# Second projection of a fused kernel: its first weight pieces are loaded one block earlier and split ahead of the latents' normalisation

## The reference

```
h = x * (1.0 + sc1) + sh1
p = h @ w_in[i]
mla_o = mla_group(p[..., :MLA_IN], cos, sin, ...)          # MLA_IN = 416
rwkv_o, v_i = rwkv7_group(p[..., MLA_IN:], ...)            # 1792 features
mix = jnp.concatenate([mla_o, rwkv_o], axis=-1) @ w_o[i]
x = layer_norm(ALPHA * x + (1.0 + gt1) * mix, ...)
x = layer_norm(ALPHA * x + (1.0 + gt2) * moe_ffn(h2, ...), ...)
```

## Time and profile before

| | us |
|---|---|
| median of three runs | 1998.43 |
| lowest, highest | 1998.28, 2002.58 |
| the profiled execution's own time | 1993.24 |
| its span, first to last instruction | 1991.5 |
| end of the entry block, PE's last instruction | 438.8 |
| second projection, from there to PE's last instruction | 438.8 to 562.3 |

### The profile page before, as it was taken

How to read it: one execution, slowest core, us unless ns; L and a number is a source line. 1 busy time by engine, 2 the same in 40 slices (tenths; PEclk the granted TensorE clock), 3 DMA queues, 4 the chain that set the end, 5 groups by cost and what they waited for, 6 DMA issues and landing times.

```text
span 1991.5 us, 27259 instructions
## 1 busy us (share of the span) xinstructions
PE 1887.4 (95%) x9418; PEld 1507.1 (76%) x9418; DVE 1576.8 (79%) x1614; ACT 1212.8 (61%) x1246; POOL 437.3 (22%) x381
## 2 busy tenths in 40 slices
PE   7999989988999879799999999999999999999997
PEld 6766656775767677788888888888888888888884
DVE  5763353773466569889999999999999999999996
ACT  5545564423464322367777777777777777777773
POOL 4535543010053332241111111111111111111110
PEclk9999998999999899799999999999999999999999
DMA  7535442414101023689999999999999999999994
GB/s 204 167 111 186 138 143 78 163 34 105 53 1 33 22 86 130 241 315 377 389 398 389 399 396 391 392 381 397 380 398 392 384 393 381 399 384 399 387 371 156
DMA packets 180403, 525.08 MB, mean 264 GB/s; under 512 B 34531, under 2 KB 52019, under 8 KB 180339
## 3 DMA queue, kind: packets, MB, share of 16 engines
q1 hardware_dynamic: 156882, 458.27, 60.5%
q0 software_dynamic: 21376, 65.95, 11.5%
q10 hardware_dynamic: 2080, 0.01, 0.1%
HBM read 499.06 MB, written 25.12 MB: 263 GB/s over the span
## 4 chain that ended last, share of the span: by engine, by line
PE 57%; DVE 2%; issue 0%; POOLq 0%; POOL 0%; DVEq 0%
PE banks L3419 53%; PE banks L3407 3%; PE banks L3413 1%; PE banks L3483 0%; DVE expert_weights L3757 0%; DVE x_tokens L3753 0%; DVE weights_lo L3553 0%; DVE x_tokens L3764 0%; DVE x_tokens L3636 0%; PE banks L3540 0%; PE banks L3504 0%; PE banks L3474 0%; DVE u_lo L3589 0%; DVE rows_lo L3583 0%; DVE member L3616 0%
## 5 line engine op out<-in xcount | busy, mean ns | idle before, releaser
L3553 DVE TENSOR_TENSOR weights_lo<-expert_weights,weights_hi 128x2048 fp32r<-128x2048 f32 x384 | 876.7, 2288 | 65.9 <-ACT weights_hi L3793 61.9
L3793 ACT ACTIVATE weights_hi<-expert_weights 128x2048 fp32r<-128x2048 f32 x384 | 738.6, 1926 | 264.2 <-PE banks L3419 252.0
L3419 PE MATMUL banks<-weights_hi,rows_hi 128*128 128x512 f32 x1024 | 319.1, 393 | 0.0
L3419 PE MATMUL banks<-weights_hi,rows_lo 128*128 128x512 f32 x1024 | 315.5, 389 | 0.0
L3419 PE MATMUL banks<-weights_lo,rows_hi 128*128 128x512 f32 x1024 | 273.8, 389 | 0.0
L3419 PEld LDWEIGHTS banks<-weights_hi,rows_hi 128*128 128x128 f32 x1024 | 189.8, 188 | 44.9 <-issue 7.3
L3419 PEld LDWEIGHTS banks<-weights_hi,rows_lo 128*128 128x128 f32 x1024 | 192.3, 188 | 40.4
L3419 PEld LDWEIGHTS banks<-weights_lo,rows_hi 128*128 128x128 f32 x1024 | 192.3, 188 | 39.9
L3419 PE MATMUL banks<-weights_hi,u_hi 128*128 128x512 f32 x512 | 160.9, 395 | 1.4 <-DVE u_lo L3589 1.4
L3419 PE MATMUL banks<-weights_hi,u_lo 128*128 128x512 f32 x512 | 157.9, 390 | 0.0
L3419 PE MATMUL banks<-weights_lo,u_hi 128*128 128x512 f32 x512 | 136.9, 389 | 0.0
(11 more groups left out here) (608 smaller groups left out, 2824.0 us busy)
## 6 DMA issues: line engine op xcount, KB each, us to landing
expert_weights<-in_exp_w SPq DMA_DIRECT2D x384, 1024.0 KB, 10.3
enter_rows<-in_ada_w POOLq DMA_DIRECT2D x24, 1024.0 KB, 5.7
w_in_landing<-in_w_in SPq DMA_DIRECT2D x16, 384.0 KB, 3.2
second_landing<-in_w_in SPq DMA_DIRECT2D x12, 512.0 KB, 3.6
x_tokens<-in_x SPq DMA_DIRECT2D x8, 512.0 KB, 6.2
w_in_landing<-in_w_in SPq DMA_DIRECT2D x8, 512.0 KB, 3.6
rwkv_room<-in_w_o SPq DMA_DIRECT2D x8, 512.0 KB, 7.6
w_in_landing<-in_w_in SPq DMA_DIRECT2D x12, 256.0 KB, 3.8
```

The lines of the kernel that those rows point to most:

```text
L3419: last = nc.tensor.matmul(c.banks[:, bank + n, :], left[:, 2 * q + kk, :], right[:, q, kk * FF + n * 512:kk * FF + (n + 1) * 512], start=s ...
L3553: nc.vector.tensor_tensor(w_lo[:, ch % SPLIT, :], c.raw[:, ch % RAW if place is None else place, :], w_hi[:, ch % SPLIT, :], ALU.subtract) ...
L3793: nc.scalar.activation(w_hi[:, ch % SPLIT, :], c.raw[:, ch % RAW if place is None else place, :], ACT.Copy).then_inc(hi_ready.sem, 1)
```

## The change

The entry block's SP list gets a wait for `products` at 8 and then issues pieces 0 to 3 of the second projection. Their landing place is set aside at a fixed address; each of the two places takes two 256 KB pieces side by side, and there are four semaphores instead of two. In the second projection, SP issues w_uv, w_uk and then pieces 4 to 15; the four loads of w_uq move to the end of POOL's loads, with a semaphore of their own, and the first value waits for w_uv and w_uk alone. PE's ten unused products go, and quarter 0 comes first; the latents are given after m = 7, and every later use six quarters later than before (values after 9, 11, 13, 15 instead of 3, 5, 7, 9, and so on to the norms after 46 to 52). ACT runs `high(0)` to `high(3)` ahead of the root. DVE runs `low(0)` to `low(2)` ahead of the sums of squares and `low(3)` between these and the reciprocal. The wait for mu moves in ACT's list to m = 6. The rope tables move to m = 14 (DVE) and 15 (ACT), arranging to m = 16, spreading to m = 18.

```diff
+                if entering:
+                    ahead_of = after["under_way"]
+                    sp.wait_ge(products.sem, 2 * TT)
+                    for n in range(4):
+                        sp.dma_start(ahead_of["place"](n), ahead_of["piece"](n)).then_inc(ahead_of["landed"][n].sem, 16)
...
-    uses = ([("latent", 2, "act", -1), ("latent", 0, "act", -1), ("latent", 1, "dve", -1)] +
-            [("value", t, ("act", "dve")[t % 2], 3 + 2 * t) for t in range(TT)] +
-            [("key", i, ("dve", "act")[i % 2], 11 + 2 * i) for i in range(4)] +
-            [("sine", 0, "act", 19), ("cosine", 0, "act", 20)] +
-            [("query", i, ("dve", "act")[i % 2], 22 + 2 * i) for i in range(4)] +
-            [("turn_a", 0, "dve", 30), ("turn_b", 0, "dve", 31), ("key_turn", 0, "act", 33),
-             ("turn_a", 1, "dve", 35), ("turn_b", 1, "dve", 36)] +
-            [("norm", t, "act", 40 + 2 * t) for t in range(TT)])
+    uses = ([("latent", 2, "act", 7), ("latent", 0, "act", 7), ("latent", 1, "dve", 7)] +
+            [("value", t, ("act", "dve")[t % 2], 9 + 2 * t) for t in range(TT)] +
+            [("key", i, ("dve", "act")[i % 2], 17 + 2 * i) for i in range(4)] +
+            [("sine", 0, "act", 25), ("cosine", 0, "act", 26)] +
+            [("query", i, ("dve", "act")[i % 2], 28 + 2 * i) for i in range(4)] +
+            [("turn_a", 0, "dve", 36), ("turn_b", 0, "dve", 37), ("key_turn", 0, "act", 39),
+             ("turn_a", 1, "dve", 41), ("turn_b", 1, "dve", 42)] +
+            [("norm", t, "act", 46 + 2 * t) for t in range(TT)])
...
-                load(0)
-                load(1)
                 sp.dma_start(uv, A["w_uv_2"].rearrange("a k n -> (a k) n")).then_inc(up_in.sem, 16)
                 sp.dma_start(uk, A["w_uk_2"].rearrange("a k n -> (a k) n")).then_inc(up_in.sem, 16)
-                for k in range(2):
-                    sp.dma_start(uq_nope[:, k, :].rearrange("p (h d) -> p h d", h=NH), uq_dram[:, k, :, 0:NOPE]).then_inc(up_in.sem, 16)
-                    sp.dma_start(uq_rope[:, k], uq_dram[:, k, :, NOPE:QK]).then_inc(up_in.sem, 16)
-                for n in range(2, pieces):
+                for n in range(4, pieces):
                     load(n)
...
+                for k in range(2):
+                    pool.dma_start(uq_nope[:, k, :].rearrange("p (h d) -> p h d", h=NH), uq_dram[:, k, :, 0:NOPE]).then_inc(uq_in.sem, 16)
+                    pool.dma_start(uq_rope[:, k], uq_dram[:, k, :, NOPE:QK]).then_inc(uq_in.sem, 16)
...
-                for _ in range(10):
-                    nc.tensor.matmul(c.banks[:, 0, :], hT[:, 0, 0, 0:P], hT[:, 0, 0, :], start=True, stop=True)
-                for u, use in enumerate(uses):
-                    if use[3] < 0:
-                        give(u)
...
+                for n in range(4):
+                    high(n)
                 act.wait_ge(sums.sem, 1)
                 nc.scalar.activation(stat[:, 1], stat[:, 0], ACT.Sqrt).then_inc(roots.sem, 1)
-                high(0)
-                high(1)
...
-                    if b == 1 and n + 2 < pieces:
+                    if b == 1 and 4 <= n + 2 < pieces:
                         high(n + 2)
                     if q == 3:
+                        if m == 6:
+                            act.wait_ge(mu_in.sem, 16)
                         previous(offset[g] + b, b)
-                    if m == 4:
+                    if m == 15:
...
+                for n in range(3):
+                    low(n)
                 for t in range(TT):
                     v.tensor_tensor_reduce(out=junk[:, t, :], ...
...
                 v.tensor_scalar(stat[:, 0, 1, :], ...).then_inc(sums.sem, 1)
+                low(3)
                 dve.wait_ge(roots.sem, 1)
...
-                    if m == 3:
+                    if m == 14:
                         tables()
-                    if m == 7:
+                    if m == 18:
                         spread_tables()
                         rotate_key()
```

More of the change, by code:

```diff
@@ L1783, in output_pieces, with second_pieces, piece, place @@
                 landed=[Signal(nc, f"leave_weights_{n}_in", 16) for n in range(OUT_PIECES)])
-def second_projection(c, A, hT, lat, raw, qT, kT, v_tok, flat, small, later, done_with):
+SECOND_GROUPS = ((3 * RP, 2), (RP, 4), (0, 4), (2 * RP, 4))
+SECOND_LANDING = 76800
+def second_pieces(nc, w_in, free):
+    def piece(n):
+        g, q = divmod(n, 4)
+        f0, width = SECOND_GROUPS[g][0] * P, SECOND_GROUPS[g][1] * P
+        return w_in[:, 2 * q:2 * q + 2, MLA_IN + f0:MLA_IN + f0 + width]
+    def place(n):
+        g = n // 4
+        width = SECOND_GROUPS[g][1] * P
+        at = n // 2 * width if g == 0 else 0
+        return landing[:, n % 2, :, at:at + width]
+    landing = nc.alloc_sbuf_tensor_at("second_landing", [P, 2, 2, 512], F32, offset=free + SECOND_LANDING)
+    return dict(piece=piece, place=place, offset=free + SECOND_LANDING,
+                landed=[Signal(nc, f"second_weights_{i}_in", 16) for i in range(4)])
+def second_projection(c, A, hT, lat, raw, qT, kT, v_tok, flat, small, later, under_way, done_with):
     nc = c.nc
@@ L1814, in second_projection @@
     RAWS, PLACES = 2, 3
-    landed = [own(f"weights_{i}_in", 16) for i in range(RAWS)]
+    landed = under_way["landed"]
     mu_in, gain_in, pos_in, up_in = own("mu_in", 16), own("latent_g_in", 16), own("positions_in", 16), own("w_up_in", 16)
+    uq_in = own("w_uq_in", 16)
     hi_ready, lo_ready, used, products = own("weights_high"), own("weights_low"), own("pieces_used"), own("products")
@@ L1850, in sb @@
             return ctx.enter_context(nc.sbuf_tensor("second_" + what, shape, dt))
-        landing = sb("landing", [P, RAWS, 2, 512])
+        assert nc.sbuf_base == under_way["offset"], (nc.sbuf_base, under_way["offset"])
+        sb("landing_room", [P, RAWS, 2, 512])
+        landing = under_way["place"]
         parts = sb("parts", [P, PLACES, 2, 2, 512], F32R)
@@ L1875, in load @@
                 def load(n):
[L1876 to L1882, removed]
-                load(0)
-                load(1)
+                    sp.wait_ge(lo_ready.sem, n - RAWS + 1)
+                    sp.dma_start(landing(n), under_way["piece"](n)).then_inc(landed[n % 4].sem, 16)
                 sp.dma_start(uv, A["w_uv_2"].rearrange("a k n -> (a k) n")).then_inc(up_in.sem, 16)
                 sp.dma_start(uk, A["w_uk_2"].rearrange("a k n -> (a k) n")).then_inc(up_in.sem, 16)
-                for k in range(2):
-                    sp.dma_start(uq_nope[:, k, :].rearrange("p (h d) -> p h d", h=NH), uq_dram[:, k, :, 0:NOPE]).then_inc(up_in.sem, 16)
-                    sp.dma_start(uq_rope[:, k], uq_dram[:, k, :, NOPE:QK]).then_inc(up_in.sem, 16)
-                for n in range(2, pieces):
+                for n in range(4, pieces):
                     load(n)
@@ L1943, in give @@
                         if i == 0:
-                            pe.wait_ge(up_in.sem, 16 * 6)
+                            pe.wait_ge(up_in.sem, 16 * 2)
                             pe.wait_ge(by_act.sem, 1)
@@ L1996, in high @@
                     width = groups[g][1] * P
-                    act.wait_ge(landed[n % RAWS].sem, 16 * (n // RAWS + 1))
+                    act.wait_ge(landed[n % 4].sem, 16 * (n // 4 + 1))
                     if n >= PLACES:
@@ L2025, in arrange @@
                 def arrange():
-                    act.wait_ge(up_in.sem, 16 * 6)
+                    act.wait_ge(uq_in.sem, 16 * 4)
                     for k in range(2):
@@ L2059, in take @@
                     last.then_inc(by_act.sem, 1)
+                for n in range(4):
+                    high(n)
                 act.wait_ge(sums.sem, 1)
                 nc.scalar.activation(stat[:, 1], stat[:, 0], ACT.Sqrt).then_inc(roots.sem, 1)
[L2063 to L2068 removed]
                 for m in range(end):
                     n, g, q, b = quarters[m]
[L2071 removed]
+                    if b == 1 and 4 <= n + 2 < pieces:
                         high(n + 2)
                     if q == 3:
+                        if m == 6:
+                            act.wait_ge(mu_in.sem, 16)
                         previous(offset[g] + b, b)
[L2075 removed]
+                    if m == 15:
                         act.wait_ge(angles.sem, 1)
                         nc.scalar.activation(ang[:], ang[:], ACT.Sin).then_inc(sines.sem, 1)
[L2078 removed]
+                    if m == 16:
                         arrange()
@@ L2186, in _ @@
                 last.then_inc(normed.sem, 1)
-                low(0)
-                low(1)
-                for u, use in enumerate(uses):
-                    if use[3] < 0 and use[2] == "dve":
-                        take(u)
                 dve.wait_ge(mu_in.sem, 16)
@@ L2209, in _ @@
                             take(u)
-    return [s.sem for s in signals]
+    return [s.sem for s in signals + landed]
 def rwkv_small(nc, ctx):
```

17 lines of the change are left out of this document (7 added, 10 removed).

## The result

The changed kernel takes 1984.84 us (median of six runs, 1978.26 to 1987.7); the kernel before took 1996.99 beside it (1993.96 to 2002.58). The ratio is 0.9932, with a 95% interval from 0.9919 to 0.9945: some 13.6 us or 0.7% faster. Forecast were 12.1 us and 1986.3. Measured again with the last group of experiments, the same kernel gave 1984.78 and a ratio of 0.9929 (0.9912 to 0.9945).

What follows compares the result with a forecast made beforehand. PE was taken as the bound, losing time in four waits and a slow stretch at the second projection's start. Gross 14.1 - 1.2 - 0.6 - 0.2 = 12.1 us, so 1998.43 - 12.1 = 1986.3 us, range 1981.5 to 1991.5.

Steps and rivals of the forecast that it cites:

- Start: PE at the projection's start: the whole stream starts 4.4 us earlier, at about 440.5 instead of 444.86.
- Holes 2 to 4 and the slow stretch: PE's waits for w_uq (3.1 us), piece 2 (0.8), first group's evacuation (3.6), and products at half clock (1.6): all go.
- the tails: Modelled product ends before PE's four waits, 0.16 us each: the waits are together 0.6 us longer than shown.
- At m = 8: PE waits 1.2 us (1.0 to 3.4) for bank 0's evacuation by ACT and DVE, with piece 5 landing at 451.2.
- the modelled end: PE's waits are measured from a modelled product end 0.16 us behind the step (0.39 against 0.235).
- At m = 24: PE waits 0.6 us more (0 to 1.0) for ACT's and DVE's chain with table load and tanh.
- At the end: Last `previous` copies end later because norm 3's sigmoid and table load fall between them: 0.2 us (0 to 0.5).
- A: Rival: the clock falls at the block's start without the unused products, costing 1.6 us; 1987.9 us; chance 0.12.
- B: Rival: piece 5 or mu comes late, making the stall before quarter 8 3.4 us; 1988.5 us; chance 0.15.
- C: Rival: piece 5 far later; slower than before if it lands after 464, say 2003 us; chance 0.02.
- hole 4: PE's two waits at the projection's start, 3.6 us, for the first group's banks, while DVE made rope tables.
- D: Rival: freed waits come back elsewhere through DVE's and ACT's fixed lists, 4 us of them; 1990.4 us; chance 0.08.

Runs made afterwards that it cites:

- the turned order: Changed kernel with DVE's `shifted` ahead of `low` wherever both stand at the same m; median 1976.7 us, ratio 0.9896 to the kernel before.
- the doubled wait: Changed kernel with piece 5 asked for only when `low(4)` is done, instead of `low(3)`; block time 116.4 us against 112.1.
- the filled experiment: Changed kernel with rope tables early, plus twelve unused products in PE's wait behind the latents' transposes; median 1985.28 us, ratio 0.9939 to the kernel before.

## Why the prediction was right, point by point

**Start, 4.4 us.** From the unused products' end to the first useful product: before 444.86 - 438.80 = 6.06, now 1.69; 4.4. Right.

**Holes 2 to 4 and the slow stretch, 9.7 with the tails.** All gone: the rows above show none of them, and the clock is 1.00 from 436 through 470. Right in sum. What the steps didn't say is how much of it is shared: w_uq's move brings 2.3 alone and 7.6 as the last part, the tables 5.3 as the last part, the early landing 9.4. They add up to more than the whole: each part alone leaves or brings a standstill at the same place, m = 8, and most of them the half clock with it.

**At m = 8, 1.2 us.** Measured 1.09, and 0.16 of the modelled end. The chain is that of the working:

```profile
452.57 0.69 ACT L2032 ACTIVATE rwkv_raw<-banks,second_mu 128x511 f32<-128x511 f32 x1 [3.14 <-PE banks L1949]
453.16 1.05 ACT L2026 ACTIVATE second_parts<-second_landing 128x1024 fp32r<-128x1024 f32 x1
```

```profile
454.24 1.23 DVE L2114 TENSOR_TENSOR second_parts<-second_landing,second_parts 128x1024 fp32r<-128x1024 f32 x1 [2.94 <-ACT second_parts L2026]
455.38 1.41 DVE L2122 SCALAR_TENSOR_TENSOR rwkv_raw<-banks,second_one_less_mu,rwkv_raw 128x512 f32<-128x512 f32 x2
```

These are ACT's and then DVE's rows of the changed kernel: `previous(0)`, `high(5)` at once behind it, so piece 5 was there (it cost nothing); then `low(5)`, and `shifted(0)` only behind it. Piece 5 was issued at 446.96 and so took at most 6.2 us. The 6.3 that I took was a guess, and the 0.2 of the 1.2 that stood on it came true by luck: `previous(0)` started at 452.57, while the working, moved by the 1.92 us that the entry block ended later, has 452.2. DVE waited 0.61 for mu, hidden, as said. That the order on DVE and not the transfer is the cause, the turned order shows.

**At m = 24, 0.6 us more.** Measured 0.96, with the 0.16 of the modelled end 1.12, where the kernel before had some 0.2 (its quarter 24 took 3.53 us for 3.36): 0.9. The working has a slip here. Its own chain gives 6.6 + 0.1 = 6.7 us against PE's 5.9, so 0.8, where before it was 6.1 against 6.1; the 0.6 that it takes follows from neither. The chain is right, by two experiments: without the table load and tanh the wait is gone, and with `shifted(2)` ahead of `low(9)` too. The term was 0.3 too small, within its range of 0 to 1.0.

**At the end, 0.2 us.** From the last unused products' start to the next block's first product: before 562.63 - 560.45 = 2.18, now 2.42. Right.

**Sum.** 12.1 forecast, 11.7 in the profile's block time, 12.2 between the medians (1996.99 - 1984.84), 13.6 by the ratio. From the rows, 4.4 + 9.7 - 1.25 - 0.9 - 0.2 gives the 11.7: the 0.4 by which the forecast is above it is mostly the term of m = 24.

**The rivals.** A, the clock falling at the start, didn't come in any of the nine profiles with the early landing and nothing in the gap, and five unused products in the gap changed nothing. B and C had the right path, and the doubled wait showed it, but the wrong price: I wrote one for one. The standstill itself does grow one for one, but behind the long ones come 1.4 to 2.4 us more. In C, too, the old time is reached with piece 5 landing at 451.0 + 12.3 = 463.3, not at 464. In the same way hole 4's 3.6 is too low a price for the tables in their old place: there they cost 5.3. (The prediction used the 3.6 for their new place, m = 14, should the cover fail there; no run tests that.) The missing step is that I took the slow stretch of the kernel before as something that goes away with two holes, not as a price that a long hole can carry with it. Here that step cost nothing since the forecast had no such hole. It did cost in the expectations: the four kernels in which a part was undone or stood alone came out 1.6 to 5.5 us above what I expected, and the half clock costs 1.7 to 3.9 us in each. D didn't come: m = 40 and the turns at 41 and 42 have no wait.

**The total of one execution.** 1993.24 - 12.1 = 1981.1 would have been the forecast for the profile; it came out at 1987.7. Nothing in the working was wrong by that much: 1.9 us were lost in the entry block and 4.4 behind the projection, where the thirteen profiles scatter by 8. That is the reason to set the range by the scatter of the runs, and the measured six lie from 1978 to 1988, one of them below the range of 1981.5 to 1991.5.

## What to carry to other kernels

Put the work that another engine waits for (evacuating a bank) ahead of the work that only has to be ready later (splitting the next piece) wherever a fixed list holds both: here that alone was worth 2.5 us more, as block time. Keep loads in many short rows off the queue that feeds the pipeline, and let a step wait only for loads that it reads. (The first was worth 7.6 us here as the last part; the second was only changed together with it.) And price a long standstill of the matrix engine with what can follow it: the wait, and the products behind it at half clock; undoing one part of a change shows this, a sum of parts doesn't.

## What the runs showed of the hardware

**The granted clock behind a standstill.** Five experiments had standstills of 3.48, 4.05, 4.26, 4.42, 4.97 and 7.00 us ahead of quarter 0 or 8. After every one of them the next twelve products took 4.48 to 5.46 us (3.04 at full clock), or 48 took 13.00 for 11.46, the first of them at a granted clock of 0.50, 1.2 GHz. After 1.09, 1.52, 1.69, 3.13 and 3.20 they ran at full pace, 2.4 GHz. The kernel before had the half clock after 3.11 and 0.77 us with one value between. The length of the standstill alone doesn't decide it: in the entry block, at one and the same place, the clock fell behind 2.06 and 2.17 us and held behind 2.01, 2.09 and 2.10, in five profiles with the same products around it. What decides there stays open, and the 3.4 us that one expectation names is no limit that a run shows. Keeping PE busy within the wait kept the clock (the filled experiment). The Trainium skill (TensorE: Matmul & The Clock Gate, Part 1: The HAM clock gate) says that the throttled state is the default, that it comes back after idling, and that only sustained activity releases it. The traces agree, and put the price here at 1.4 to 2.4 us a time.

**Strided loads on SP and on POOL.** In the changed kernel POOL issues the four w_uq loads in 0.88 us each, and they land in 5.8 and 6.4 us:

```profile
h_mix<-in_w_uq POOLq DMA_DIRECT2D x2, 256.0 KB, 5.8
h_mix<-in_w_uq POOLq DMA_DIRECT2D x2, 128.0 KB, 6.4
```

On SP the last two took 1.81 and 2.83 us to issue, and the piece behind them, in rows of 2 KB, at least 9 us to land, with 10.0 as the longest transfer of that profile. The Trainium skill (DMA: Bandwidth & Descriptors, Issuing engine by pattern) calls the queues of SP and ACT generally faster than POOL's. For these rows of 128 and 256 bytes no run here shows that: from issue to landing they took 6.5 to 8.4 us on SP and 4.2 to 6.4 on POOL, at other moments and beside other transfers. What mattered here was who stands behind them in the list.
